# Six norms of a two-layer trunk: the squares of the input summed by TensorE from eight buffers instead of on GpSimd

## The reference, cut to what matters

```python
def rmsnorm(x, g):
    xf = x.astype(jnp.float32)
    y = xf * lax.rsqrt(jnp.mean(xf * xf, axis=-1, keepdims=True) + RMS_EPS)
    return (y * g.astype(jnp.float32)).astype(x.dtype)
...
        h = rmsnorm(x, g[0])
        x = x + 0.5 * rmsnorm(swiglu(h, ...), g[1])
        h = rmsnorm(x, g[2])
        u = h @ prm['w_in'][l]
...
```

## Time and profile before

| | |
|---|---|
| median of 3 runs | 2847.99 us (2843.57 to 2848.58) |
| profiled execution | 2846.76 us, its span 2845.0 us |
| TensorE busy, weight loads busy | 2671.6 us (94%), 2608.1 us (92%) |
| VectorE, ScalarE, GpSimd busy | 992.7, 758.7, 906.7 us |
| mean granted clock of TensorE | 0.963 of full speed |
| line 527, additions of squares on GpSimd | 84, 78.7 us |
| line 1454, one-column matmuls | 180 instructions |

### The profile page before, as it was taken

One profiled execution on the slowest core, in us unless ns is written; L12 is line 12 of the kernel. 1 busy time (PEld: TensorE's weight loads), 2 busy tenths in 40 slices (PEclk: granted clock), 3 DMA queues, 4 the chain that ended last, 5 costly groups with the idle time before them and its releaser, 6 DMA issues.

```text
span 2845.0 us, 48369 instructions
## 1 busy us (share of the span) xinstructions
PE 2671.6 (94%) x20910; PEld 2608.1 (92%) x20910; DVE 992.7 (35%) x1486; ACT 758.7 (27%) x1067; POOL 906.7 (32%) x444
## 2 busy tenths in 40 slices
PE   6999999899889899999989999999988899999997
PEld 5999999898679799999989999998977789999997
DVE  5222201675554622210152221027655553222103
ACT  3222211322422322221232222123133133222211
POOL 4333333333112433333243333334321033333331
PEclk8999999999799999999999999999987999999998
DMA  3222222223102222222212222222230022222221
GB/s 99 67 74 74 72 75 76 65 67 91 34 3 54 59 74 74 74 70 76 77 51 74 75 74 71 74 78 58 67 94 9 2 68 67 74 74 74 75 73 61
DMA packets 356052, 188.37 MB, mean 66 GB/s; under 512 B 16330, under 2 KB 354086, under 8 KB 355912
## 3 DMA queue, kind: packets, MB, share of 16 engines
q1 hardware_dynamic: 355668, 186.25, 22.5%
q10 hardware_dynamic: 244, 0.08, 0.0%
HBM read 179.50 MB, written 6.80 MB: 65 GB/s over the span
## 4 chain that ended last, share of the span: by engine, by line
PE 88%; DVE 7%; DVEq 2%; issue 2%; ACT 1%; ACTq 1%; POOL 1%; POOLq 0%
PE ps L1435 27%; PE ps L1437 26%; PE ps L1436 26%; PE ps L1429 1%; DVE h_split L969 1%; DVE xT L962 1%; PE ps L1875 1%; PE ps L1859 1%; PE ps L1871 1%; PE ps L1454 1%; DVEq L961 1%; POOL w_lo L523 1%; PE ps L1586 0%; DVE ps L960 0%; PE ps L1694 0%
## 5 line engine op out<-in xcount | busy, mean ns | idle before, releaser
L523 POOL TENSOR_TENSOR w_lo<-w_raw,w_hi 128x1024 fp32r<-128x1024 f32 (+1 forms) x330 | 787.1, 2387 | 1607.9 <-ACT w_hi L589 1604.8
L1435 PE MATMUL ps<-h_split,w_hi 128*128 128x384 f32 (+1 forms) x3808 | 1208.8, 317 | 66.0 <-POOL w_lo L523 44.8
L1437 PE MATMUL ps<-h_split,w_lo 128*128 128x384 f32 (+1 forms) x3808 | 1191.6, 313 | 0.0
L1436 PE MATMUL ps<-h_split,w_hi 128*128 128x384 f32 (+1 forms) x3808 | 1183.0, 311 | 0.0
L1435 PEld LDWEIGHTS ps<-h_split,w_hi 128*128 128x128 f32 x3808 | 724.5, 190 | 79.1 <-POOL w_lo L523 41.8
L1437 PEld LDWEIGHTS ps<-h_split,w_lo 128*128 128x128 f32 x3808 | 730.8, 192 | 0.0
L1436 PEld LDWEIGHTS ps<-h_split,w_hi 128*128 128x128 f32 x3808 | 726.3, 191 | 1.3
L589 ACT ACTIVATE w_hi<-w_raw 128x1024 fp32r<-128x1024 f32 (+1 forms) x330 | 342.1, 1037 | 877.4 <-DMA w_raw<-in_ffn_w_down 403.7
L1435 PE MATMUL ps<-hidden_split,w_hi 128*128 128x384 f32 (+1 forms) x1344 | 419.7, 312 | 0.0
L1437 PE MATMUL ps<-hidden_split,w_lo 128*128 128x384 f32 (+1 forms) x1344 | 416.6, 310 | 0.0
L1436 PE MATMUL ps<-hidden_split,w_hi 128*128 128x384 f32 (+1 forms) x1344 | 413.2, 307 | 0.0
(11 more groups left out here) (302 smaller groups left out, 1734.8 us busy)
## 6 DMA issues: line engine op xcount, KB each, us to landing
w_raw<-in_ffn_w_gate SPq DMA_DIRECT2D x88, 512.0 KB, 3.8
w_raw<-in_ffn_w_up SPq DMA_DIRECT2D x88, 512.0 KB, 3.8
w_raw<-in_ffn_w_down SPq DMA_DIRECT2D x64, 448.0 KB, 3.8
w_raw<-in_w_in SPq DMA_DIRECT2D x42, 512.0 KB, 4.0
w_raw<-in_ffn_w_down SPq DMA_DIRECT2D x32, 512.0 KB, 4.1
w_raw<-in_w_out SPq DMA_DIRECT2D x16, 512.0 KB, 4.1
token_rows<-in_x_prompt SPq DMA_DIRECT2D x4, 512.0 KB, 5.8
k_cache<-in_cache_sb_k SPq DMA_DIRECT2D x2, 1024.0 KB, 7.3
```

What stands on the lines that cost most here:

```text
L523: nc.gpsimd.tensor_tensor(WLO[s][:, 0:n], RAW[s][:, 0:n], WHI[s][:, 0:n].bitcast(F32), ALU.subtract).then_inc(sem(f"lo_ready{s}"), 1)
L1435: MM(out, hi, mov[:, 0, cols], start=first, stop=False)
L1436: MM(out, hi, mov[:, 1, cols], start=False, stop=False)
L1437: return MM(out, lo, mov[:, 0, cols], start=False, stop=last)
```

## The change

ScalarE writes the squares of all eight chunks into a buffer of their own, `SQ`, `chunk_squares`, 8 x 640 numbers in each partition, which lies over the hidden rows 4 to 8 of `HID`. The waits of ScalarE for additions go, and so do the 84 additions and drains on GpSimd, whose `cross` holds only the low halves of weights. `pre_sums` waits for the eighth square instead of the seventh addition, and calls `token_sums` with eight buffers: 24 matmuls for group 0 and 16 for group 1, accumulated in PSUM. Their places in TensorE's order stay. `ACC` is written in the crossing only by `diagonal` and `rstd_kept` (and by the norm behind the sub-layer before).

```diff
+        scope = ExitStack()
+        sb("hidden_front", [P, 9 * T], stack=scope)
+        SQ = sb("chunk_squares", [P, DC, T], stack=scope)
+        scope.close()
...
-            def add_squares(p, g, k):
-                pool.wait_ge(sem(f"squares{g}"), p * DC + k + 1)
-                nc.gpsimd.tensor_tensor(ACC[:, GROUPS[g]], ACC[:, GROUPS[g]], SCR[:, k % 2, GROUPS[g]], ALU.add)
-                pool.drain().then_inc(sem(f"squares_summed{g}"), 1)
-
             def cross(p):
                 b0 = first_block(p)
                 after = {2: 2, 4: 3} if p % 3 == 2 else ({2: 1, 4: 2, 5: 3} if p else {1: 0, 2: 1, 4: 2, 5: 3})
-                for k in range(1, DC):
-                    add_squares(p, 0, k)
-                    if k in after:
-                        low(b0 + after[k])
-                for k in range(1, DC):
-                    add_squares(p, 1, k)
+                for q in after.values():
+                    low(b0 + q)
...
-                if k >= 3:
-                    act.wait_ge(sem(f"squares_summed{g}"), p * (DC - 1) + k - 2)
-                A(SCR[:, k % 2, GROUPS[g]] if k else ACC[:, GROUPS[g]], XT[:, c, GROUPS[g]], ACT.Square).then_inc(sem(f"squares{g}"), 1)
+                A(SQ[:, k, GROUPS[g]], XT[:, c, GROUPS[g]], ACT.Square).then_inc(sem(f"squares{g}"), 1)
...
-                pe.wait_ge(sem(f"squares_summed{g}"), (p + 1) * (DC - 1))
-                token_sums(PRE_SUMS[g], g, (ACC,)).then_inc(sem(f"norm_sums{g}"), 1)
+                pe.wait_ge(sem(f"squares{g}"), (p + 1) * DC)
+                token_sums(PRE_SUMS[g], g, [SQ[:, k, :] for k in range(DC)]).then_inc(sem(f"norm_sums{g}"), 1)
```

## The result

| | before | changed |
|---|---|---|
| median | 2845.81 us (4 runs, 2843.57 to 2848.58) | 2922.51 us (4 runs, 2916.05 to 2924.3) |
| profiled execution, its span | 2846.76, 2845.0 us | 2916.05, 2914.0 us |
| mean granted clock | 0.963 | 0.953 |

The changed kernel is slower: ratio 1.0265, 95% interval 1.0244 to 1.0286, or 77 us. The forecast was 2920 us, range 2885 to 2938.

What follows compares the result with a forecast made beforehand. TensorE, busy 94% of the span and 88% of the chain, was taken as the bound. Sums +47.0, additions' removal -4 and lower clock +29 gave +72 on 2848, so 2920 us, range 2885 to 2938.

Steps and rivals of the forecast that it cites:

- The 47.0 us of sums: TensorE in the six crossings: 420 more sum instructions at 0.112 us each, all on the path, +47.0 us.
- the whole tail: Behind group 1's sums: everything moves back with them, and TensorE's 6.00 us idle behind FFN crossings can't absorb the sums.
- The rival of cheap sums: Sums on TensorE: loads overlap with neighbours, 0.07 us an instruction, 29 us in all, 2873 us; chance 0.04.
- that of hidden loads: Two runs per crossing: sums' loads hide fully under neighbouring products, only the 4 us gain remains, 2844 us; chance 0.03.
- The clock: TensorE's granted clock falls in most long runs of sums, slowing sums and following products, +29 us; likeliest case, chance 0.60.
- 18.5 us on group 0: Group 0's runs of 48: clock falls 3.2 us into a run, 3.7 us lost in five of six crossings.
- 10.4 on group 1: Group 1's runs of 32: slower sums and 24 slower products behind, 2.6 us in four of six crossings.
- the rival of a clock that holds: TensorE's long runs of sums: clock stays at 1.00, so only +43 us, 2891 us; chance 0.33.
- The additions' removal: GpSimd's 78.7 us of additions in the crossings, nearly all hidden: removal gains 4 us, bounds 14 gained to 3 lost.
- The restart in crossing 0: TensorE's restart at 30.06 us comes 1.5 us sooner without the addition before the second block's subtraction, at 28.5.
- h_low's mean: VectorE's h_low steps in the crossings: mean below 904 ns but far above 0.6 us after the change.
- The page's floor: Skill's 25 ns per short matmul, without its load: sums would cost 10.5 us, 2854 us in all; set aside for the trace.

Runs made afterwards that it cites:

- the kernel with one buffer: Changed kernel, but sums taken of the eighth square buffer only, so no additions and no extra sums; 2838.54 us, ratio 0.997 to the kernel before.
- the two-pass sums: Kernel before, additions on GpSimd kept, but TensorE takes its sum eight times from the same summed buffer; 2921.4 us, ratio 1.0258.

## Why the prediction was right, point by point

**The 47.0 us of sums: right.** 420 instructions came, at 0.112 us each wherever the clock was full (0.67 us for six between products). All were on the path: the whole tail moved and its 6.00 us stayed. The rival of cheap sums and that of hidden loads are out: the two-pass sums cost 73 us by themselves, and spreading them didn't hide their loads.

**The clock: right in kind and sum, wrong in its parts.** I put 18.5 us on group 0 (3.7 us in five of six crossings) and 10.4 on group 1 (2.6 in four). It fell in all six crossings and for both groups. The lower level lasts 6.8, 6.8, 6.8, 10.2, 10.2 and 6.8 us at group 0's runs, 47.8 us in all, and 3.4 us at each of group 1's, 20.5 in all. At 0.45 us lost in each these are 21.5 and 9.2, 30.7 in sum against my 29.

For group 0 one fall costs 3.6 us, as reckoned. It came 3.9 us into a run in the mean, not 3.2, so fewer sums were slow (3.0 us of them where I had 4.2), and products stayed slow for 3.4 to 6.1 us where I had taken 3 to 5. Only the count was wrong, six falls for five. For group 1 one fall costs 1.5 us and not 2.6: it came 4.2 us behind the start of a run that lasts 3.7, and the clock was back after 3.4 us, while I had let all 24 products behind the run be slow. Here six falls came for four. That too few falls and too dear ones cancelled is luck. The place of the fall was in part luck too. I took it from the earlier trace rows, where TensorE had idled for 2.47 us shortly before, as the timeline of TensorE in the kernel before shows:

```profile
2131.59 1.09 PE L1429 MATMUL ps<-consts,sig 128*128 128x128 f32 x8 [2.47 <-DVEq L1266]
```

So that row couldn't tell a run of small matmuls from a pause. The twelve runs, which have no idle time in them, can.

Against the kernel with one buffer the spans give 2914.0 - 2839.2 = 74.8 us, less 47.0 leaves 27.8. So the rival of a clock that holds (2891) fell, by about the difference that spreading the same sums out made (2889).

**The additions' removal: somewhat too small.** I put -4 us. TensorE's waits fell by 3.4 for the low halves and 2.5 for h_low, 5.9 us. The restart in crossing 0 came at 28.3 (I wrote 28.5), but only 1.3 of its 1.8 us were its own wait. The medians without the added sums give 8.5 (6 to 11), the profiles 5.8, of which 5.4 stand in the attention stages; so more than the 5.9 us of waits is not shown to be the additions'. I had stepped through the crossings and believed the subtractions would meet other h_low steps as badly; h_low's mean fell from 904 to 805 ns, so they don't quite. That VectorE and GpSimd slow each other stands in the Trainium skill, SBUF — State Buffer, "Who interferes with whom", and these means agree. What this gain should have brought next to the long runs was not seen: additions kept or not, both kernels take 2921 to 2923 us. The intervals reach 5 to 6 us to each side, and which part of the 8.5 is lost was not settled.

**The sum.** 2846 + 47 + 31 - 6 = 2918, against 2914.0 to 2916.05 in the profile and 2922.5 in the median; the profiled execution was the fastest of its four. I forecast 2920.

**The page's floor.** The Trainium skill's TensorE: Matmul & The Clock Gate, "Back-to-back issue gap", gives 25 ns for a matmul of 1 to 64 columns; by it the sums would have cost 10.5 us. The runs give 0.112 us each. Every one brings its own load of 128 columns, and the profile shows loads without a gap through the runs; that the load sets the price fits this, and no run takes the load away to show it. With one instruction for a call the kernel was 57 us faster, and with the ones as weights 81 us.

## What to carry to other kernels

Work moved from an engine with slack to the one that sets the end must be cheap there: count its instructions with their weight loads, and let the long side move, since sixteen matmuls with ones as weights did in 2.4 us what eighty instructions with one column did in 9 and a lowered clock. If short matmuls can't be avoided, put a few at a time among long ones, best where the engine would wait anyway; expect a wider scatter, since the clock then holds in most places and not in all. And ask first which result the idle time behind a stage hangs on: producing it three chunks sooner, without a change in the work, was worth 27 us in the medians, of which the profiles place some 20 in the crossings, most of it the pauses themselves. Before you explain a small difference, compare stages that the change doesn't touch: here they alone differ by up to 7.6 us.

## What the runs showed of the hardware that was not expected

- The clock of a fully busy TensorE fell at all twelve long runs of one-column sums, 3.0 to 4.9 us behind their starts, and stayed down for 3.4 to 10.2 us. The six products between two runs of 24 did not prevent it. With runs of 12 and as many products between, it fell in two of six crossings of the profiled execution, behind the fourth run; with runs of 6 and 8 it fell in none of that kernel's profile, and once among runs of 6, behind a wait of 0.78 us, in the kernel that spreads group 0 alone.
- TensorE can be busy throughout and stay at the lower clock: 33 us at 0.50, with runs of six sums between every six products behind a slow restart. Executions of that kernel scatter by 29 us (2886.04 to 2915.44).
- A float32 matmul of one column cost the same 0.112 us for each of its two instructions in runs of 6, of 12 (2.39 us from run to run, less 6 x 0.175) and longer; only the clock changed it (0.21 at the lower level, (39.16 - 35.96 - 6 x 0.32)/6).
